# One layer of a hybrid S5, attention and expert mixer on one core: six pages in rotation, the last modulation weights loaded before the gather stream, and a quarter of the prompt's early expert rows summed on VectorE

## The reference

```python
sh1, sc1, g1, sh2, sc2, g2 = silu(cvec) @ w_mod + b_mod      # 12 column blocks of 512
h  = rmsnorm(x, norm1) * (1 + sc1) + sh1
u, c_q, c_kv, k_rope = split(h @ w_in)                        # S5 mixer on u, attention on the rest
x  = x + g1 * (concat(ssm_out, attn) @ w_out)
h2 = rmsnorm(x, norm2) * (1 + sc2) + sh2
# peer: 8 heads x 16 picks of 16384 experts for every token
q = h2 @ w_query; s = q . sub_keys; top_s, top_i = top_k(s, 16)      # two tables of 128 keys per head
best_s, pos = top_k(top_s[0] + top_s[1], 16); idx = ...; g = softmax(best_s)
act = gelu(h2 . u_table[idx]) * g
y   = sum over the 128 picks of act * v_table[idx]
x   = x + g2 * y
out = rmsnorm(x, final_norm)
```

## Time and profile before

| | us |
|---|---|
| median of 3 runs (933.15 to 936.01) | 933.62 |
| the profiled execution | 927.89 |
| its span, first to last instruction | 926.1 |

### The profile page before, as it was taken

The page is one execution under the profiler, slowest core; times in us unless marked ns, Lnnn a source line. Parts: engine busy times, 40 slices in busy tenths (PEclk is TensorE's granted clock), DMA queues, the critical chain, the costliest instruction groups (busy, mean ns, idle before and its releaser), DMA issues. The chain is left out here.

```text
span 926.1 us, 11524 instructions
## 1 busy us (share of the span) xinstructions
PE 757.3 (82%) x4033; PEld 382.6 (41%) x4033; DVE 560.0 (60%) x1230; ACT 341.8 (37%) x1005; POOL 361.9 (39%) x335
## 2 busy tenths in 40 slices
PE   3898889965897799979999868974984988598875
PEld 0676565732363335546764223321421432242221
DVE  7978212533466644683594579559757855965444
ACT  3412251232562435234244336333432533343331
POOL 4339500022243245314437434642652554264420
PEclk9999999987998799979999998997998999799998
DMA  9954375355999499977999999999999999999992
GB/s 369 378 210 164 106 286 215 110 212 234 421 366 337 146 410 419 422 282 279 424 406 380 423 421 423 420 423 422 420 422 421 421 423 421 423 419 423 421 421 122
DMA packets 45665, 320.95 MB, mean 347 GB/s; under 512 B 5340, under 2 KB 6044, under 8 KB 7592
## 3 DMA queue, kind: packets, MB, share of 16 engines
q0 software_dynamic: 36864, 268.45, 71.1%
q1 hardware_dynamic: 8376, 51.59, 14.2%
q10 hardware_dynamic: 368, 0.18, 0.1%
HBM read 318.97 MB, written 1.23 MB: 346 GB/s over the span
## 5 line engine op out<-in xcount | busy, mean ns | idle before, releaser
L800 PE MATMUL psum<-mem 128*128 128x512 f32 x1024 | 504.6, 629 | 128.6 <-ACT mem L1172 128.0
L1778 DVE CUSTOM_DVE_ANT_0 mem<-mem,h 128x1024 f32<-128x1024 f32 x256 | 309.0, 1224 | 253.1 <-DMA mem<-uv_table,small 249.5
L1445 POOL DMA_INDIRECT mem<-uv_table,small x256 | 294.3, 1150 | 422.8 <-PE psum L800 320.8
L800 PEld LDWEIGHTS psum<-mem 128*128 128x128 f32 x1024 | 187.8, 197 | 403.8 <-ACT mem L1172 229.2
L1165 ACT ACTIVATE small<-small 128x1 f32<-128x1 f32 x256 | 51.4, 201 | 314.5 <-DVE small L1778 308.8
L1172 ACT ACTIVATE mem<-consts,small 128x128 f32<-128x128 f32 x256 | 102.8, 401 | 8.7
L1168 ACT ACTIVATE small<-small 128x1 f32<-128x1 f32 x256 | 75.4, 294 | 25.3 <-ACT small L1165 1.9
L747 PEld LDWEIGHTS psum<-hT,mem 128*128 128x128 f32 x480 | 59.3, 195 | 15.6 <-issue 15.6
L747 PE MATMUL psum<-hT,mem 128*128 128x128 f32 x480 | 59.5, 278 | 1.3 <-ACT mem L1088 1.3
L1368 POOL TENSOR_SCALAR small<-small 128x1 f32<-128x1 f32 (+1 forms) x9 | 4.2, 472 | 101.7 <-DVE small L1677 57.7
L991 ACT COPY late<-psum 128x512 f32<-128x512 f32 (+3 forms) x39 | 21.2, 569 | 36.6 <-PE psum L782 18.4
(11 more groups left out here) (216 smaller groups left out, 657.5 us busy)
## 6 DMA issues: line engine op xcount, KB each, us to landing
mem<-w_mod SPq DMA_DIRECT2D x24, 1024.0 KB, 8.5
mem<-w_query SPq DMA_DIRECT2D x8, 1024.0 KB, 8.9
mem<-w_out SPq DMA_DIRECT2D x4, 1024.0 KB, 8.1
mem<-uv_table,small POOLq DMA_INDIRECT x256, 17.8
mem<-w_in_u SPq DMA_DIRECT2D x2, 1024.0 KB, 14.9
mem<-w_in_qkv SPq DMA_DIRECT2D x2, 1008.0 KB, 11.9
mem<-w_ukv SPq DMA_DIRECT2D x1, 1024.0 KB, 8.6
mem<-w_glu SPq DMA_DIRECT2D x1, 1024.0 KB, 5.2
```

The lines of the kernel that those rows point to most:

```text
L800: mm = pe.matmul(bank(f"acc_{g}_{half}"), diag[:, pick % DEEP, :], row_of(pick)[:, D + 512 * half:D + 512 * half + 512], start=first, stop ...
L1445: pool.indirect_dma_start(row_of(pick), None, uv_table, bass.IndirectOffsetOnAxis(ap=idx[:, pick:pick + 1], axis=0)).then_inc(row_landed[R ...
L1778: dve.tensor_tensor_reduce(out=row[:, 0:D], in0=row[:, 0:D], in1=h[:, pick // PICKS, :], scale=1.0, scalar=0.0, op0=ALU.mult, op1=ALU.add, ...
```

## The change

Six edits, which belong together:

- `mod2b.0` to `mod2b.3` now go through pages 15, 3, 15, 3. The four pair steps stand ahead of the sample's latents: step 0 before `normed_turned(0)`, steps 1 and 2 between the first queries and scores of the prompt, step 3 after `turned_back`. ACT copies `mq2b` to `brow` ahead of pick 0, and `spread_row("g2")` reads it there.
- `query1.0` is loaded to page 6 (the page of `uq`) instead of page 3, and so page 6 is not a gather page until pick 70.
- The steps 1 to 7 of the sample's latents come after pair step 3, and both halves of the S5 part of the output projection after them, ahead of `hlast` (before, the second half was in picks 1 and 2).
- `free` is `[15, 3, 4, 5, 2, 13]`; pages arrive at picks 12 (0), 36 (15), 70 (6), 71 (7), 82, 83, 88. From pick 1 on five pages rotate until pick 11 and six from pick 12 on (before: six from pick 6), seven from pick 36 (before: 34).
- ACT does `latent_squares(1)` in pick 0 and `latents_scaled(1)` in pick 2; POOL's inverse root comes after the gather of pick 4 instead of 3.
- The 24 picks 1, 5, 9, ... 93 (`ADDED`) are not accumulated by PE. DVE adds weight times row to `side` (two rows of `modrow`) with one instruction of 128x1024 (`add_row`), after the product of the next pick; it waits for ACT's weight of that pick. ACT writes no diagonal for them. Their page is released by `row_added` instead of `row_free`. `add_experts(0)` adds `side` to the sum, one DVE instruction of 128x512 more in each half.

```diff
 PAGES += [("mod2a.0", 15), ("mod2a.1", 8), ("out1.1", 14), ("out1.0", 13), ("mod2a.2", 9), ("mod2a.3", 15), ("query0.0", 8), ("query0.1", 9)]
-PAGES += [(f"mod2b.{i}", 3) for i in range(4)]
-PAGES += [("query1.0", 3), ("query1.1", 7), ("query2.0", 1), ("query2.1", 14), ("query3.0", 8), ("query3.1", 9)]
+PAGES += [(f"mod2b.{i}", (15, 3)[i % 2]) for i in range(4)]
+PAGES += [("query1.0", 6), ("query1.1", 7), ("query2.0", 1), ("query2.1", 14), ("query3.0", 8), ("query3.1", 9)]
 ORDER = {name: n for n, (name, _) in enumerate(PAGES)}
 SCORED = [0, 0, 1, 2, 4, 5, 3, 6, 7]
...
 def row_plan():
-    free = [15, 4, 5, 2, 13]
-    arriving = {5: 0, 6: 6, 34: 15, 68: 3, 69: 7, 82: 1, 83: 14, 88: 8}
+    free = [15, 3, 4, 5, 2, 13]
+    arriving = {12: 0, 36: 15, 70: 6, 71: 7, 82: 1, 83: 14, 88: 8}
     rows, before, uses, queue = [], [], [], [(p, None) for p in free]
...
     return rows, before, uses
+
+
+ADDED = [pick for pick in range(96) if pick % 4 == 1]
+
+
+def summed_rank(pick):
+    return pick + 1 - added_rank(pick)
+
+
+def added_rank(pick):
+    return sum(p <= pick for p in ADDED)
 def bank_plan():
...
         g1b = [late[:, 0:1024], late[:, 3072:4096]]
         tmpB = [late[:, 1024:2048], yb[:, 512:1536]]
+        side = modrow[:, 0:3:2, :]
         g2b = late[:, 2048:4096].rearrange("p (g n) -> p g n", g=G)
         fnb, out2 = late[:, 4096:5120], late[:, 5120:6144]
...
         row_landed = {p: sem(f"row{p}_landed") for p in sorted(set(ROW))}
-        dots_ready, gel_ready, wts_ready, diag_ready, row_free = (
-            sem(n) for n in ("dots_ready", "gel_ready", "wts_ready", "diag_ready", "row_free"))
+        dots_ready, gel_ready, wts_ready, diag_ready, row_free, row_added = (
+            sem(n) for n in ("dots_ready", "gel_ready", "wts_ready", "diag_ready", "row_free", "row_added"))
         sqf_ready, rstdf_ready, y_out_ready, stored = sem("sqf_ready"), sem("rstdf_ready"), sem("y_out_ready"), sem("stored")
         ckv_stored, ssm_stored = sem("ckv_stored"), sem("ssm_stored")
...
                 out = start(name)
-                mm = pe.matmul(out, column.to_broadcast([P, P]), modrow[:, 0 if v == "g2" else n // 4, :], start=True, stop=True)
+                mm = pe.matmul(out, column.to_broadcast([P, P]), brow[:, :] if v == "g2" else modrow[:, n // 4, :], start=True, stop=True)
                 finish(mm, name)
             def transposes(name, sources, rows=P):
...
                         start(f"acc_{g}_{half}")
-                pe.wait_ge(diag_ready, pick + 1)
+                pe.wait_ge(diag_ready, summed_rank(pick))
                 for half in range(2):
...
             gate_projection(1, (0, 1, 2, 3))
+            pair_step("b", 0)
+            normed_turned(0, 0)
+            normed_turned(0, 1)
             pe.wait_ge(y_read, NC)
             latents(1, (0,))
-            normed_turned(0, 0)
-            normed_turned(0, 1)
-            latents(1, (1,))
             first_queries()
-            latents(1, (2,))
+            pair_step("b", 1)
             first_scores(0)
             second_queries()
-            latents(1, (3,))
+            pair_step("b", 2)
             first_scores(1)
...
             turned_back(0, 1)
-            pair_step("b", 0)
-            latents(1, (4, 5, 6, 7))
-            pair_step("b", 1)
-            out_projection(1, 0, range(4), first=True)
+            pair_step("b", 3)
+            latents(1, (1, 2, 3, 4, 5, 6, 7))
+            for half in range(2):
+                out_projection(1, half, range(4), first=True)
             finish(pe.transpose(start("hlast")[0:2 * DT, 0:P], hlast, ident), "hlast")
             for pick in range(PICKS * G):
-                if pick in (1, 2):
-                    out_projection(1, 1, range(2 * pick - 2, 2 * pick), first=pick == 1)
-                elif pick == 3:
+                if pick == 3:
                     latents_turned(1)
...
                     attention_keys(1, (pick - 6) // 2, "kv"[pick % 2])
-                    if pick in (6, 8):
-                        pair_step("b", pick // 2 - 1)
                 elif pick == 10:
...
                 elif pick in (13, 14, 15, 16):
-                    if pick == 13:
-                        wait_emptied(pe, "mq2b")
                     attention_scores(1, pick - 13)
...
                 elif pick in (104, 105, 106, 107):
+                    if pick == 104:
+                        wait_emptied(pe, "mq2b")
                     spread_row("g2", (pick - 104) // 2, pick % 2)
-                accumulate(pick)
+                if pick not in ADDED:
+                    accumulate(pick)
         @block.scalar
...
                 act.wait_ge(gel_ready, pick + 1)
+                if pick - DEEP in ADDED:
+                    act.wait_ge(row_added, added_rank(pick - DEEP))
                 act.activation(wts[:, cut_], gel[:, cut_], ACT.Copy, scale=gate[:, pick:pick + 1]).then_inc(wts_ready, 1)
+                if pick in ADDED:
+                    return
                 act.wait_ge(wts_ready, pick + 1)
-                if pick >= DEEP:
-                    act.wait_ge(row_free, pick - DEEP + 1)
+                if pick >= DEEP and pick - DEEP not in ADDED:
+                    act.wait_ge(row_free, summed_rank(pick - DEEP))
                 act.activation(diag[:, slot, :], ident, ACT.Copy, scale=wts[:, cut_]).then_inc(diag_ready, 1)
             act.wait_ge(consts_here, 16)
...
             back_evac(0)
+            evacuate(brow[:, :], bank("mq2b"), "mq2b")
             soft_exp(1, 0, TOPK)
-            latent_squares(1)
-            latents_scaled(1)
             wait_filled(act, "hlast")
...
             for pick in range(PICKS * G):
                 weigh(pick)
-                if pick == 3:
+                if pick == 0:
+                    latent_squares(1)
+                elif pick == 2:
+                    latents_scaled(1)
+                elif pick == 3:
                     latents_evac(1)
...
                     key_evac(1, 1)
-                    evacuate(modrow[:, 0, :], bank("mq2b"), "mq2b")
                 elif pick == 9:
...
                     if pick == 0:
-                        pool.wait_ge(mod_used, 20)
+                        pool.wait_ge(mod_used, MOD.index("mod2b.2") + 1)
                     else:
                         wait_filled(pool, "at1")
+                elif page_ == 3:
+                    pool.wait_ge(mod_used, MOD.index("mod2b.3") + 1)
                 elif page_ in (4, 5):
...
                     pool.wait_ge(out_used, 1 + (2, 13).index(page_))
-                elif page_ in (0, 6):
+                elif page_ == 0:
                     wait_filled(pool, "q_1_1")
-                elif page_ in (3, 7):
+                elif page_ in (6, 7):
                     wait_filled(pool, "qry_1_1")
...
                     available(ROW[pick], pick)
+                elif ROW_BEFORE[pick] in ADDED:
+                    pool.wait_ge(row_added, added_rank(ROW_BEFORE[pick]))
                 else:
-                    pool.wait_ge(row_free, ROW_BEFORE[pick] + 1)
+                    pool.wait_ge(row_free, summed_rank(ROW_BEFORE[pick]))
                 pool.indirect_dma_start(row_of(pick), None, uv_table,
                                         bass.IndirectOffsetOnAxis(ap=idx[:, pick:pick + 1], axis=0)).then_inc(row_landed[ROW[pick]], 16)
...
             for pick in range(PICKS * G):
                 gather(pick)
-                if pick == 3:
+                if pick == 4:
                     inverse_root(rstd_a[:, 2:4], ms_a[:, 2:4], [(0, 1, QR), (1, 2, KVR)], sqa_ready, 4, rstda_ready)
...
                                          accum_out=dots[:, slot:slot + 1]).then_inc(dots_ready, 1)
+            def add_row(pick):
+                rank = added_rank(pick)
+                dve.wait_ge(wts_ready, pick + 1)
+                row = row_of(pick)[:, D:2 * D].rearrange("p (a n) -> p a n", a=2)
+                weight_ = wts[:, pick % DEEP:pick % DEEP + 1]
+                if rank == 1:
+                    ins = dve.tensor_scalar(side, row, weight_, None, ALU.mult)
+                else:
+                    dve.wait_ge(row_added, rank - 1)
+                    ins = dve.scalar_tensor_tensor(side, row, weight_, side, ALU.mult, ALU.add)
+                ins.then_inc(row_added, 1)
+
             def add_experts(g):
...
                     wait_filled(dve, name)
-                    empties(dve.tensor_tensor(out2[:, cut_], bank(name), g2b[:, g, cut_], ALU.mult), name)
-                    wait_emptied(dve, name)
+                    if g == 0:
+                        dve.wait_ge(row_added, len(ADDED))
+                        empties(dve.tensor_tensor(out2[:, cut_], bank(name), side[:, half, :], ALU.add), name)
+                        wait_emptied(dve, name)
+                        tt(out2[:, cut_], out2[:, cut_], g2b[:, g, cut_], ALU.mult)
+                    else:
```

(4 more changed lines are left out.)

## The result

The changed kernel takes 902.25 us (median of 4 runs, 898.14 to 902.62), the kernel before, on the same chip, 934.49 (933.15 to 936.01). The ratio is 0.9645, 95% interval 0.9612 to 0.9677. The forecast was 903.6, range 891 to 920. The profiled execution after took 902.62 us, its span is 900.8.

The account below looks back on a forecast made before the run. The DMA engines' gathers at 421 GB/s were taken as the bound. Loads, start, head, first search and 393 to 509 us summed to -36.5; 6.5 allowed back gave -30, median 903.6 us, range 891 to 920.

Parts of the forecast that it names:

- Modulation loads: Before the stream of gathers: three weight loads no longer share the stream's DMA time, 3 x 2.49, -7.5 us.
- The start: Ahead of the first gather: `normed_turned` stands behind a pair step instead of a latent step, +0.6 us.
- The head: First gathers, 181 to 231 us: gather 5 goes at 201.7 instead of 218.72, loss 7.7 instead of 22.6, -14.9 us.
- The search of unit 1: 255 to 324 us: VectorE's search starts at about 258 without waiting for scores, loss 16 instead of 22.8, -6.8 us.
- Picks 50 to 90: Forecast as 393 to 509 us: added picks relieve a full TensorE, loss 10.5 instead of 18.4, -7.9 us.
- allowance of 6.5 for uneven rows: Added to the whole sum because the three new losses, laid out by hand, are least values: -36.5 becomes -30 us.
- The first (916.6): Whole stream: only head and loads pay, TensorE's relief buys nothing, late pages cost about 5; -17 us, chance 0.20.
- The second (892): Whole stream: everything fits, no uneven rows and the search gaps halve; -41.5 us, chance 0.12.
- The third, the clock: Picks 36 to 96: TensorE idles more and may sit at its lower clock; about -20 us, 913.6, chance 0.06.
- The fourth (955): Added picks up to 69: their pages come back too late, 18 gaps of 3.2 us; +21 us, chance 0.06.
- The fifth: Head: `hlast` or the inverse root slips a further 15 us, its gain is gone; about -15, 918, chance 0.04.
- The rule against the change: GpSimd's gathers: VectorE instructions with two SBUF inputs hold them; 24 more holders, 29 us if all on the path.

Follow-up runs that it names:

- experiment 3: The kernel before with only the 24 picks summed on VectorE, nothing else of the change; 923.26 us, ratio 0.9891.
- adds_only: The kernel of experiment 3: the kernel before with only the 24 picks summed on VectorE; 923.26 us, ratio 0.9891.
- head_only: The changed kernel with no added picks, so TensorE sums all 256; 914.20 us, ratio 0.9805 to the kernel before.
- second pair of profiles: The kernel before and the changed kernel, each run and profiled once more without edits; 932.59 us and 902.22 us.
- unsearched: The changed kernel without VectorE's search of unit 1, gates and indices copied from unit 0; 888.34 us, ratio 0.9498 to the kernel before.
- experiment 11: The run unsearched: the changed kernel without VectorE's search of unit 1; 888.34 us, ratio 0.9498 to the kernel before.

## Why the prediction was right, step by step

**Right in size.** -32.2 us between the medians against -30 forecast; -32.7 in stream time against a raw sum of -37.1 (the -36.5 without the start's +0.6). The terms, from the first pair of profiles:

- Modulation loads: -7.5 as forecast; the fourth issue of that row's `x4` is over at 180.09 (158.82 + 21.27). The bound written for it, before 175, was missed, in an execution whose stream starts 7.4 us later; it still lies 8 us ahead of the stream.
- The start: +0.6 forecast. From TensorE's start of the gate projection (159.87 before, 166.45 after) to gather 0 it is 21.04 us before and 21.84 after, +0.8. The other 6.6 of the later start arose ahead of any changed code, and go with the clock of 0.87 instead of 1.00 from 80 to 120 us (experiment 3). So it belongs to the executions.
- Gather 5: forecast 20.2 us behind gather 0 (201.7 - 181.5), measured 20.1 (208.40 - 188.29), through the chain that was forecast: GpSimd waits 6.05 for ACT's squares. By the letter the prediction's own sign of being wrong, gather 5 after 206, came true (208.40); it had tied the sign to the clock of one execution.
- The adds: 1.285 us each for the 1.24 taken by the nearest row; the loss of 64-90 fell from 10.8 to 2.0, where the full TensorE stood. In adds_only it fell to 3.5, in head_only it stayed, so the adds did it.
- 24 fewer picks took 504.6 - 457.4 = 47.2 us off the line that sums them, for the 43 of the sum. TensorE's whole busy time fell by 35 only, since ahead of the stream, where the clock was lower in this execution, it rose from 153.1 to 160.8.

**Mis-sized.** *The head*: -14.9 forecast, -11.6 measured (22.6 to 11.0). The new loss is 10.8 to 11.4 in the seven profiles with this head, for 7.7 forecast. Of these 3.3 us 2.0 are a slip of counting: the old loss counts from the issue of gather 0, the new gaps were counted from the first bytes 2 us later. The second pair of profiles has -14.8 for the head (26.0 to 11.2), so the old loss was itself taken low. *The search of unit 1*: -6.8 forecast, -2.6 measured (22.6 to 20.0; the second pair has 20.6 to 20.5), the step that failed most. I had the search begin at 258 by taking TensorE's freed 11 us and the earlier stream off it. It began 84.2 us behind gather 0 (272.44 - 188.29) and not 76.5, for two links that I left out: TensorE's queries stood behind ACT's exponentials,

```profile
256.51 5.44 PE L759 MATMUL psum<-hT,mem 128*128 128x128 f32 x32 [3.50 <-ACT mem L1097]
```

and VectorE waited 5.48 us for ACT's weight of pick 21 ahead of its add, a wait between engines that the change itself brings. Even so these were not the cost: in unsearched the same add waits 5.3 us and the stretch loses 6.4. The stretch is bound by VectorE's work, and that grew: its window from gather 22 to 40 is this in head_only, which has no adds,

```profile
249.59:322.24 72.65, 56.88 (x203) 31.46 (x204) 43.76 (x114) 28.36 (x81) 18.65 (x18) 0.86 0.75 274
```

and 47.49 instead of 43.76 in the changed kernel (experiment 11). So three things met there: with the earlier stream alone it lost 25.4, 2.8 or 4.8 more than in the two profiles of before; with TensorE's relief on top 5.4 less (20.0); and five adds of 1.28 stand in the way of more. The first two numbers are near the scatter of single profiles, so their split is likely and not shown. I counted the relief in full and the other two hardly at all. My reading of the ground for it was also off: VectorE was busy 40%, 67% and 53% in the three windows of the earlier trace rows from 181 to 393, not 60 to 70%, and it was the search, not the mean, that mattered. *Picks 50 to 90*: -7.9 forecast for 393 to 509; measured (7.3 + 10.8) - (5.6 + 2.0) = -10.5, more than forecast. Together the errors are 3.3 + 4.2 - 2.6 = 4.9 us too much gain, which the allowance of 6.5 for uneven rows covered; that its size was near was luck, for its reason was not the one that the runs show. The piece 12-22, forecast at nothing, gave 1.0 more.

**Signs.** Of those written down, these held:

- 23 adds near 1.24;
- gather 60 some 5 us behind its place in the row (3.2 behind the start of product 54, which ran at 376.33, instead of 1.7 ahead of it);
- a tail of 19.1;
- no wait of GpSimd on VectorE that repeats at every fourth pick: of the 12 only 3.58 (at 257.81) and 3.04 (at 340.98) pass 3 us besides the two in the searches.

These did not:

- the search of unit 1 began at 272.44 and not between 256 and 264;
- from gather 5 to 250 us it is 388 GB/s and not 400, from 216 on 421;
- 391 to 415, the former 416 to 440, has 383 and not 390;
- the last gather goes 26.0 us earlier and not 30 (33.4 in stream time).

**Rivals.** The first (916.6) falls with adds_only. The second (892) fails at the search. The third, the clock: 0.79 from 264 to 312, where TensorE has 33.00 of 48 us to do and VectorE is the limit, 1.00 from 416 to 484; unsearched has 0.96 in the former place. From 271.29 to 295.41 VectorE's products wait for no data, so a faster TensorE would not have brought them earlier there; its cost by itself no run separates. The fourth (955) falls: GpSimd waits 34.4 us in 12 waits on the adds, and the stretches between the searches run at 419 to 422 GB/s. The fifth falls with gather 5.

**The rule against the change.** One gather of the changed kernel took 1.88 us from 208.40, against 0.94 for its neighbours, and VectorE's timeline has a product beside it until 209.36:

```profile
208.15 1.21 DVE L1797 CUSTOM_DVE_ANT_0 mem<-mem,h 128x1024 f32<-128x1024 f32 x1
```

The 0.94 us more is about what was left of the product (0.96). It is no single case. Of the 256 gathers of this trace 71 are issued while a VectorE instruction of 128x1024 has 0.25 to 1.2 us to run, and they take 1.09 to 1.99 us, each 0.80 to 0.92 more than what was left. Of the 151 issued under none the median is 0.94, and two take over 1.2. Among these are 93 during which such an instruction starts; none of them takes over 1.05, so a gather that has begun is not held. The Trainium skill (SBUF — State Buffer, "Who interferes with whom") says that a VectorE instruction with two SBUF inputs contends with a GpSimd instruction that reads SBUF, and the trace agrees. With 23 more such instructions the stream still moves 419 to 422 GB/s between the searches, so here the rule costs nothing where GpSimd runs ahead.

## What to carry to other kernels

Where a stream of transfers is the bound, count losses in bytes at its own top rate from its first transfer on, and compare pieces cut at transfers, not at times: the first transfer's time moved by 5.4 us here under unchanged code, with the clock granted to TensorE ahead of it, more than most edits are worth. A gain ahead of a stretch that another engine bounds can be given back in it; ask of each edit which engine's amount of work it changes there, and try once without that work before reordering around it. A wait that a page of the profile shows in front of a gather (7 and 9 us here) can cost far less than its length, when the engine that reads the rows is behind anyway.

## What the runs showed of the hardware that was not expected

An add of a row times a weight per partition to 128x1024 floats takes 1276 to 1321 ns in 23 cases, some 60 ns more than the product's 1224. Its first, without a sum to add to, took 0.77; VectorE's timeline of the changed kernel:

```profile
207.46 0.77 DVE L1807 TENSOR_SCALAR modrow<-mem,small 128x1024 f32<-128x1024 f32 x1 [4.71 <-ACT small L1179]
```

Nor did I expect the same code ahead of the stream to take 5.4 us more in one execution than in another, and the granted clock from 80 to 120 us, 1.00 in the one and 0.91 in the other, to go with it; the times of the kernel before, of seven runs on one chip, spread from 929.27 to 937.34. The gathers that a VectorE instruction already running held (above) are the third: up to 1.99 us instead of 0.94, and none where the gather was first.
